# In-projection summed over two halves of K instead of four quarters, with the modulation tiles reordered to match

## The chip, the cores and the metric

The kernel runs on one core of a Trainium2 chip. Its time is the device time of one execution in microseconds. The five engines run side by side and meet through semaphores: TensorE (PE in the rows), VectorE (DVE), ScalarE (ACT), GpSimd (POOL) and SyncE (SP), which here only issues DMAs.

## What is computed

One layer of a hybrid encoder with S = 256 tokens and D = 2048, batch 1, all in float32. The parts that matter here:

```python
c_act = jax.nn.silu(c)
mod = c_act @ w_ada[l] + b_ada[l]                       # (1, 6 * 2048)
sh_a, sc_a, g_a, sh_m, sc_m, g_m = [m[:, None, :] for m in jnp.split(mod, 6, axis=-1)]
h = rms_norm(x, norm_mix[l]) * (1.0 + sc_a) + sh_a
p = h @ w_in[l]                                         # the in-projection, K = 2048
...                                                     # latent projections, three attentions
x = x + g_a * (o @ w_out[l])
h = rms_norm(x, norm_ffn[l]) * (1.0 + sc_m) + sh_m
x = x + g_m * (jnp.square(jax.nn.relu(h @ w_ff1[l])) @ w_ff2[l])
```

## The kernel before

Every large weight comes as **units** of 128 x 1024 floats (512 KB): two K tiles by 512 columns. Four buffers (`RING`) hold raw units, four their high parts, four their low parts. SP loads a unit into `raw`; ACT (`hi`, L334) rounds it to `w_hi`; VectorE (`lo`, L594) subtracts to get `w_lo`; TensorE (`unit`, L975 and L981) multiplies `w_hi` with the high and low half of the operand and `w_lo` with the high half, 24 matmuls, and counts `unit_used`. ACT may overwrite `w_hi` of a unit once TensorE has used the unit four before it, and SP may overwrite `raw` once VectorE has done `lo` of the unit four before it (`lo_done`).

The modulation vector `mod` isn't made by TensorE. VectorE makes it from `w_ada`, in 192 **tiles** of 128 x 1024 (`ada_tile`, L606), each a multiply by `c_rep` (silu(c) on all partitions) and a sum along the row; two tiles give one column of `mod`. The tiles too pass through four buffers (`ADA`): SP may load tile a once tile a - 4 is done (`ada_done`), and VectorE waits for the tile's landing (`ada_full`). VectorE takes the tiles in a fixed order, between its other work. Tiles 0 to 63 are scale and shift of the mixer, 64 to 95 the mixer's gate (first needed behind the out-projection), the rest belongs to the MLP.

An operand **pair** is two K tiles of h, and needs eight tiles of `mod`: `mix_gain` and `norm_t` on VectorE (L625, L636), `mix_hi` on ACT (L360), `norm_lo` on VectorE (L647).

The **in-projection** has 64 units. K is cut into four quarters; for each quarter q there are eight column blocks b of two units. TensorE sums a block's two units in PSUM (two sets, used in turn) and VectorE adds the block to `pT` (`read_block`, L662, L663; a copy in the first quarter). Quarter q needs operand pairs 2q and 2q + 1. Ahead of the loop stand 16 tiles and two pairs (the **head**); each block carries two tiles, and pairs 2q + 2 and 2q + 3 are made in blocks 4 and 7 of quarter q. The loop thus takes 64 tiles, and 16 are left to the **latent projections** (10 units, seven blocks).

Each engine has one queue, in the order in which the functions below write it. SP's is the one that sets when loads start: a DMA whose semaphore isn't there yet holds all that stand behind it. What it waits for is in these lines:

```python
def load_unit(u):
    slot = u % RING
    if u >= RING:
        sp.wait_ge(lo_done, u - RING + 1)
def load_ada(a):
    slot = a % ADA
    if a >= ADA:
        sp.wait_ge(ada_done, a - ADA + 1)
```

Of the kernel before, what the change touches and what calls it, by code (L numbers as in the profile page):

```python
# [22 lines left out]
P = 128  # L23
D, S, FF = 2048, 256, 8192
EPS = 1e-6
KT = D // P
# [7 lines left out]
RING = 4  # L34
LAG = RING
AHEAD = LAG + RING
# [15 lines left out]
ADA = 4  # L52
SH_A, SC_A, G_A, SH_M, SC_M, G_M = range(6)


QT = KT // 4
QC = KT
A_GA, A_SHM, A_SCM, A_GM, A_END = 64, 96, 128, 160, 192


# [7 lines left out]

USE_XS = 0
USE_IN = 1  # L70
USE_LSTAT = 33
USE_LAT = 34
USE_ROT, USE_VM, USE_VS = 41, 42, 43
USE_OT = 44
USE_OUT = 46
USE_FFN = 50
USE_FF1A, USE_FF2A, USE_FF1B, USE_FF2B, USE_END = 51, 59, 63, 71, 75

READY = {use: n + 1 for n, use in enumerate((
    USE_XS, USE_LSTAT, USE_ROT, USE_VM, USE_VS, USE_OT, USE_OT + 1, USE_FFN, USE_END))}  # L80
# [2 lines left out]
R_MIX, R_CQ, R_CKV, R_O, R_FFN = 0, 8, 10, 11, 19  # L83
# [43 lines left out]
def hybrid_block(nc, xt_in, cols_in, consts_in, w_ada, weights, c_row, out):  # L127
    ctx = ExitStack()
    with ctx:
# [130 lines left out]
        @block.sync  # L260
        def _(sp):
# [4 lines that stand above are left out]
                sp.dma_start(raw[:, slot, :, :].rearrange("p k n -> p (k n)"),  # L266
                             weights[u, :, :]).then_inc(raw_full[slot], 16)
# [5 lines that stand above are left out]
                sp.dma_start(ada[:, slot, :], w_ada[a, :, :]).then_inc(ada_full[slot], 16)  # L273

            sp.dma_start(cols[:, :], cols_in).then_inc(ld_cols, 16)
            load_ada(0)
            sp.dma_start(xT[:, :, :].rearrange("p k t -> p (k t)"), xt_in).then_inc(ld_x, 16)
            load_ada(1)
            load_ada(2)
            for a in range(3, ADA):  # L280
                load_ada(a)
            for u in range(RING):
                load_unit(u)
            for a in range(8):
                load_ada(a + ADA)
            load_unit(RING)
            load_unit(RING + 1)
            for a in range(8, 12):
                load_ada(a + ADA)
            load_unit(RING + 2)  # L290
            load_unit(RING + 3)
            for a in range(12, 16):
                load_ada(a + ADA)

            for q in range(4):
                if q == 3:
                    sp.dma_start(consts[:, :], consts_in).then_inc(ld_const, 16)
                for b in range(8):
                    load_unit(QC * q + AHEAD + 2 * b)
                    load_unit(QC * q + AHEAD + 2 * b + 1)  # L300
                    for a in range(2):
                        load_ada(16 * (q + 1) + 2 * b + a + ADA)

            loaded = AHEAD
            for n in range(7):
                for u in range(loaded, LAT_ENDS[n] + 1 + AHEAD):
                    load_unit(B_LAT + u)
                loaded = LAT_ENDS[n] + 1 + AHEAD
                for a in range(2):
                    load_ada(A_GA + 16 + 2 * n + a + ADA)  # L310
            for a in range(A_GA + 30, A_SCM):
                load_ada(a + ADA)

            for j in range(U_OUT):
                load_unit(B_OUT + AHEAD + j)
                load_ada(A_SCM + j + ADA)
            for j in range(UNITS - B_FF - AHEAD):
                load_unit(B_FF + AHEAD + j)
                if j % 2 == 1 and A_GM + j // 2 + ADA < A_END:
                    load_ada(A_GM + j // 2 + ADA)  # L320
            for j in range(4):
                sp.wait_ge(result_ready, 4 * j + 4)
                src = (tmp, tmp2, sq, ssq)[j]
                sp.dma_start(out[:, 4 * j * S:(4 * j + 4) * S], scratch(src)).then_inc(ld_out, 16)
            sp.wait_ge(ld_out, 64)

        @block.scalar
        def _(sc):
            def hi(u0, step, it, j):
                slot = (u0 + j) % RING  # L330
                sc.wait_ge(raw_full[slot], 16 * ((u0 + j) // RING + 1) + (16 * step // RING) * it)
                if u0 + j >= RING:
                    sc.wait_ge(unit_used, u0 + j - RING + 1 + step * it)
                sc.activation(w_hi[:, slot, :, :], raw[:, slot, :, :], ACT.Copy).then_inc(hi_done, 1)  # L334
# [44 lines left out]
            def mix_hi(j):  # L379

                sc.wait_ge(ada_done, 8 * j + 8)
                operand_hi(R_MIX + j, hT[:, 2 * j:2 * j + 2, :, :], mod[:, SH_A, 2 * j:2 * j + 2])

            mix_hi(0)
            mix_hi(1)
            for q in range(4):
                for b in range(8):
                    hi(QC * q + LAG, 0, 0, 2 * b)
                    hi(QC * q + LAG, 0, 0, 2 * b + 1)
                    if q < 3 and b == 4:  # L390
                        mix_hi(2 * q + 2)
                if q < 3:
                    mix_hi(2 * q + 3)

            sc.wait_ge(part_done, 32)
            for i, n in ((0, 4), (1, 2)):
                if i:
                    sc.wait_ge(cq_summed, 1)
# [125 lines left out]
        def _(gp):  # L524
# [5 lines left out]
            gp.wait_ge(zeroed, 1)  # L530
            for b in range(4):
                add_squares(b + 1)
            gp.wait_ge(part_done, 32)
            gp.memset(foxA[:, :], 0.0).then_inc(fox_filled, 1)
            gp.memset(foxG[:, :], 0.0).then_inc(fox_filled, 1)
            gp.wait_ge(fox_filled, 2)
# [53 lines left out]
        def _(ve):  # L590
            def lo(u):
                slot = u % RING
                ve.wait_ge(hi_done, u + 1)
                ve.tensor_tensor(w_lo[:, slot, :, :], raw[:, slot, :, :],  # L594
                                 w_hi[:, slot, :, :].bitcast(F32), ALU.subtract).then_inc(lo_done, 1)
# [56 lines left out]
            def norm_t(r0, j):  # L652
                scaled_pair(r0 + j, xT[:, 2 * j:2 * j + 2, :], gain[:, 2 * j:2 * j + 2], 0)

            def norm_lo(r0, shift, j):
                operand_lo(r0 + j, hT[:, 2 * j:2 * j + 2, :, :], mod[:, shift, 2 * j:2 * j + 2])
# [35 lines left out]
            def mix_gain(j):  # L692
                make_gain(SC_A, C_MIX, 2 * j, 2, 8 * j + 7)
                ve.wait_ge(gain_ready, j + 1)

            for a in range(8):
                ada_tile(a)
            lo(0)
# [5 lines left out]
            ada_tile(8)  # L704
            ada_tile(9)
            invert(1, 1)
            mix_gain(0)
            norm_t(R_MIX, 0)
            ada_tile(10)
            norm_lo(R_MIX, SH_A, 0)  # L710
            ada_tile(11)
            lo(2)
            lo(3)
            for a in range(12, 16):
                ada_tile(a)
            mix_gain(1)
            norm_t(R_MIX, 1)
            norm_lo(R_MIX, SH_A, 1)

            for q in range(4):  # L720
                for b in range(8):
                    u = QC * q + 2 * b
                    lo(u + LAG)
                    lo(u + LAG + 1)
                    ada_tile(16 * (q + 1) + 2 * b)
                    ada_tile(16 * (q + 1) + 2 * b + 1)
                    if q < 3 and b == 4:
                        mix_gain(2 * q + 2)
                        norm_t(R_MIX, 2 * q + 2)
                    if q < 3 and b == 5:  # L730
                        norm_lo(R_MIX, SH_A, 2 * q + 2)
                    if q < 3 and b == 7:
                        mix_gain(2 * q + 3)
                        norm_t(R_MIX, 2 * q + 3)
                    if q:
                        ve.wait_ge(part_done, 8 * (q - 1) + b + 1)
                    read_block(pT[:, 4 * b:4 * b + 4, :], USE_IN + 8 * q + b, u + 2, add=q > 0).then_inc(part_done, 1)
                    ve.wait_ge(part_done, 8 * q + b + 1)
                    ve.sem_inc(psum_free, 1)
                    if q < 3 and b == 7:  # L740
                        norm_lo(R_MIX, SH_A, 2 * q + 3)

            ve.wait_ge(psum_ready, READY[USE_LSTAT])
            mean(USE_LSTAT, 0, 0, QL)
# [27 lines left out]
            for n, e in enumerate(LAT_ENDS):  # L772
                for u in range(LAG if n == 0 else LAT_ENDS[n - 1] + 1 + LAG, e + 1 + LAG):
                    lo(B_LAT + u)
                ada_tile(A_GA + 16 + 2 * n)
                ada_tile(A_GA + 16 + 2 * n + 1)
                read_block(dests[n], USE_LAT + n, B_LAT + e + 1).then_inc(psum_free, 1)
            ada_tile(A_GA + 30)
            ada_tile(A_GA + 31)
            ve.wait_ge(psum_free, USE_LAT + 8)  # L780

            cos, sin = consts[:, K_COS:K_COS + S], consts[:, K_SIN:K_SIN + S]
# [177 lines left out]
        def _(pe):  # L960
# [47 lines left out]
            pe.wait_ge(ld_cols, 16)  # L1008
            pe.wait_ge(ssq_done, 4)
            token_sums(USE_XS, 1, ssq, 4).then_inc(psum_ready, 1)  # L1010
            for q in range(4):
                for b in range(8):
                    product(QC * q + 2 * b, 2, USE_IN + 8 * q + b, hT, QT * q, lambda j: (op_lo, R_MIX + 2 * q + j + 1))
            take(USE_LSTAT)
            pe.wait_ge(sq_done, 5)
            token_sums(USE_LSTAT, 0, tmp2, 4).then_inc(cq_summed, 1)
# [191 lines left out]
```

## Time and profile before

| | us |
|---|---|
| median of 3 runs | 1302.89 (1298.74 to 1304.67) |
| the profiled execution | 1298.17 |
| its span, first to last instruction | 1296.4 |
| head, until the loop starts | 54.65 |
| in-projection loop | 54.65 to 283.3 |
| latent projections, statistics ahead of them included | 283.3 to 345.5 |
| TensorE busy | 1139.5 (88%) |
| VectorE busy | 903.8 (70%) |

The shares of the span are means over stages with different limits, so the stages are to be read one by one. Times in the rows are microseconds from the start of the span, durations in the last brackets are idle time of the engine ahead of that row and who ended it. A line such as "x2" joins instructions of one kind that follow one another.

### The profile page before, as it was taken

The numbers are of one execution on the slowest core, as the hardware profiler recorded it, in microseconds if no ns is written. First come the engines' busy times: TensorE is split into PE (matmuls) and PEld (weight loads), VectorE is DVE, ScalarE is ACT, GpSimd is POOL, SyncE is SP. The second block draws the span as 40 slices with busy tenths as digits, with TensorE's granted clock in tenths as the row PEclk, the third lists the DMA queues.
The fourth block names the chain that finished last, engine by engine and source line by source line (L and its number), as shares of the span: only waits on it lengthen the run. The fifth ranks groups of instructions, "written<-read, shape, count | busy, mean of one in ns | idle before, by whom it ended". The sixth has DMA issues, their size and how long they took to land.

```text
span 1296.4 us, 22085 instructions
## 1 busy us (share of the span) xinstructions
PE 1139.5 (88%) x9186; PEld 1097.1 (85%) x9186; DVE 903.8 (70%) x1172; ACT 523.0 (40%) x619; POOL 87.1 (7%) x86
## 2 busy tenths in 40 slices
PE   1497888867698969959999999999999999999996
PEld 0487877866566659949999999999999999999996
DVE  4797989878879988888777765444455555554554
ACT  3132323324167633335444443333345444444441
POOL 3000000000026520010000000000000000000000
PEclk9898989888858779979999999999999999999998
DMA  8797979884744438975878766666665666666661
GB/s 308 273 325 254 322 264 326 304 296 151 271 146 149 156 112 330 369 298 197 309 275 307 278 211 194 195 193 196 189 193 193 198 192 196 195 193 197 194 192 71
DMA packets 81170, 298.49 MB, mean 230 GB/s; under 512 B 9136, under 2 KB 9264, under 8 KB 80688
## 3 DMA queue, kind: packets, MB, share of 16 engines
q1 hardware_dynamic: 80784, 296.03, 67.6%
q8 instruction: 73, 1.20, 0.4%
q10 hardware_dynamic: 288, 1.06, 0.2%
q14 instruction: 25, 0.20, 0.0%
HBM read 294.94 MB, written 2.11 MB: 229 GB/s over the span
## 4 chain that ended last, share of the span: by engine, by line
PE 65%; DVE 22%; issue 7%; ACT 3%; DMA 2%; POOL 1%; DVEq 0%; ACTq 0%; POOLq 0%
PE ps L975 41%; PE ps L981 20%; DVE ada L606 10%; DVE w_lo L594 4%; DVE pT L662 2%; PE ps L1064 2%; ACT w_hi L334 1%; DMA c_rep<-c_row 1%; DVE pT L663 1%; DVE tmp L636 1%; DMA c_row<-c_act 1%; DVE rstd L619 1%; DVE hT L647 1%; DVE stick L830 0%; PE ps L1005 0%
## 5 line engine op out<-in xcount | busy, mean ns | idle before, releaser
L594 DVE TENSOR_TENSOR w_lo<-raw,w_hi 128x1024 fp32r<-128x1024 f32 x362 | 446.3, 1246 | 305.9 <-ACT w_hi L334 301.4
L334 ACT ACTIVATE w_hi<-raw 128x1024 fp32r<-128x1024 f32 x362 | 380.5, 1059 | 526.0 <-PE ps L981 496.3
L975 PE MATMUL ps<-hT,w_hi 128*128 128x256 f32 x3584 | 457.7, 281 | 60.4 <-DVE hT L647 22.0
L975 PEld LDWEIGHTS ps<-hT,w_hi 128*128 128x128 f32 x3584 | 433.9, 192 | 68.3 <-DVE hT L647 22.8
L975 PE MATMUL ps<-act,w_hi 128*128 128x256 f32 x2048 | 252.9, 276 | 0.0
L981 PE MATMUL ps<-hT,w_lo 128*128 128x256 f32 x1792 | 242.6, 278 | 0.4 <-DVE w_lo L594 0.4
L975 PEld LDWEIGHTS ps<-act,w_hi 128*128 128x128 f32 x2048 | 241.6, 188 | 0.0
L981 PEld LDWEIGHTS ps<-hT,w_lo 128*128 128x128 f32 x1792 | 222.9, 190 | 0.6 <-DVE w_lo L594 0.6
L981 PE MATMUL ps<-act,w_lo 128*128 128x256 f32 x1024 | 136.9, 276 | 0.0
L981 PEld LDWEIGHTS ps<-act,w_lo 128*128 128x128 f32 x1024 | 125.6, 188 | 0.0
L606 DVE CUSTOM_DVE_ANT_0 ada<-ada,c_rep,half_sum 128x1024 f32<-128x1024 f32 x96 | 123.8, 1307 | 0.3 <-DMA ada<-in_ada 0.3
L606 DVE CUSTOM_DVE_ANT_0 ada<-ada,c_rep,cols 128x1024 f32<-128x1024 f32 x64 | 84.1, 1324 | 0.0
L527 POOL TENSOR_TENSOR ssq<-ssq,sq 128x1024 f32<-128x1024 f32 x10 | 25.4, 2539 | 753.3 <-ACT sq L340 739.1
L606 DVE CUSTOM_DVE_ANT_0 ada<-ada,c_rep,plus_one 128x1024 f32<-128x1024 f32 x32 | 40.8, 1276 | 15.2 <-DMA c_rep<-c_row 15.0
L562 POOL TENSOR_TENSOR tmp<-o_tok 128x64 f32<-128x64 f32 (+1 forms) x48 | 35.7, 764 | 18.4 <-DVE o_tok L844 13.2
L975 PE MATMUL ps<-lat,w_hi 128*128 128x256 f32 x160 | 23.7, 306 | 14.8 <-issue 7.3
L975 PEld LDWEIGHTS ps<-lat,w_hi 128*128 128x128 f32 x160 | 21.9, 209 | 16.1 <-issue 7.6
L930 DVE TENSOR_TENSOR act<-tmp,act 128x1024 fp32r<-128x1024 f32 x16 | 19.6, 1225 | 18.1 <-ACT act L502 18.1
L502 ACT ACTIVATE act<-tmp 128x1024 fp32r<-128x1024 f32 x16 | 17.0, 1062 | 33.8 <-DVE tmp L924 33.8
L360 ACT ACTIVATE hT<-tmp,mod 128x256 fp32r<-128x256 f32 x16 | 8.1, 508 | 54.0 <-DVE tmp L636 54.0
L662 DVE TENSOR_TENSOR pT<-pT,ps 128x1024 f32<-128x1024 f32 x24 | 29.2, 1215 | 0.0
L994 PE MATMUL ps<-ssq,cols 128*128 128x256 f32 x8 | 3.8, 650 | 27.0 <-POOL ssq L527 27.0
(141 smaller groups left out, 625.5 us busy)
## 6 DMA issues: line engine op xcount, KB each, us to landing
raw<-in_weights SPq DMA_DIRECT2D x362, 512.0 KB, 4.4
ada<-in_ada SPq DMA_DIRECT2D x192, 512.0 KB, 5.2
xT<-in_xt SPq DMA_DIRECT2D x1, 2048.0 KB, 8.5
consts<-in_consts SPq DMA_DIRECT2D x1, 1156.0 KB, 8.1
c_rep<-c_row ACTq DMA_DIRECT2D x1, 1024.0 KB, 8.1
y<-tmp SPq DMA_DIRECT2D x2, 512.0 KB, 2.6
y<-sq SPq DMA_DIRECT2D x1, 512.0 KB, 2.6
y<-ssq SPq DMA_DIRECT2D x1, 512.0 KB, 2.6
```

Source lines behind the costliest of these rows:

```text
L334: sc.activation(w_hi[:, slot, :, :], raw[:, slot, :, :], ACT.Copy).then_inc(hi_done, 1)
L502: sc.activation(act[:, 4 * b + 8 * it:4 * b + 8 * it + 4, 0, :], tmp2[:, :, :], ACT.Copy).then_inc(act_hi, 1)
L527: gp.tensor_tensor(ssq[:, :, :], ssq[:, :, :], sq[:, :, :], ALU.add).then_inc(ssq_done, 1)
L562: ins = gp.tensor_tensor(osq[i % 2][:, q * d:q * d + d], o, o, ALU.mult)
L594: ve.tensor_tensor(w_lo[:, slot, :, :], raw[:, slot, :, :], w_hi[:, slot, :, :].bitcast(F32), ALU.subtract).then_inc(lo_done, 1)
L606: ve.tensor_tensor_reduce(out=ada[:, slot, :], in0=ada[:, slot, :], scale=1.0, scalar=first, in1=c_rep[:, half * D // 2:(half + 1) * D // ...
L619: ve.reciprocal(rstd[:, 0:halves, :], rstd[:, 0:halves, :]).then_inc(rstd_ready, 1)
L662: return ve.tensor_tensor(dst, dst, set_of(use), ALU.add)
L930: ve.tensor_tensor(act[:, 4 * it:4 * it + 4, 1, :], tmp2[:, :, :], act[:, 4 * it:4 * it + 4, 0, :].bitcast(F32), ALU.subtract).then_inc(ac ...
L975: pe.matmul(acc[:, n, :], w, rhs[:, kt0 + k, half, :], start=first and k == 0 and n % 2 == 0 and half == 0, stop=False, skip_group_check=True)
L981: ins = pe.matmul(acc[:, n, :], w_lo[:, slot, k, n * P:(n + 1) * P], rhs[:, kt0 + k, 0, :], start=False, stop=last and k == UK - 1, skip_g ...
L1064: ins = pe.matmul(s[:, q * P:(2 * q + 1) * P], lhs[:, q * P:(q + 1) * P], rhs[:, 0:(q + 1) * P], start=(m == 0), stop=(m == len(terms) - 1))
```

## The change

QT, the K tiles of a part, goes from 4 to 8: the in-projection has two halves of eight column blocks, and a block sums four units in PSUM ahead of its read. The first half needs pairs 0 to 3, so the head now has 32 tiles and four pairs; pairs 4 to 7 are made in blocks 1, 3, 5 and 7 of the first half. A block carries four tiles, one behind each unit's subtraction. The loop takes tiles 32 to 95, so none is left in the latent projections. The host packs the weights in two parts, and the counters follow.

```diff
-QT = KT // 4
-QC = KT
+QT = KT // 2
+QC = 2 * KT
@@ SP
-            for a in range(8):
+            for a in range(28):
                 load_ada(a + ADA)
-            load_unit(RING)
-            load_unit(RING + 1)
-            for a in range(8, 12):
-                load_ada(a + ADA)
-            load_unit(RING + 2)
-            load_unit(RING + 3)
-            for a in range(12, 16):
-                load_ada(a + ADA)
-
-            for q in range(4):
-                if q == 3:
+                if a % 7 == 6:
+                    load_unit(RING + a // 7)
+
+            for q in range(2):
+                if q == 1:
                     sp.dma_start(consts[:, :], consts_in).then_inc(ld_const, 16)
                 for b in range(8):
-                    load_unit(QC * q + AHEAD + 2 * b)
-                    load_unit(QC * q + AHEAD + 2 * b + 1)
-                    for a in range(2):
-                        load_ada(16 * (q + 1) + 2 * b + a + ADA)
+                    for j in range(4):
+                        load_unit(QC * q + AHEAD + 4 * b + j)
+                        load_ada(32 * (q + 1) + 4 * b + j)
...
-                for a in range(2):
-                    load_ada(A_GA + 16 + 2 * n + a + ADA)
-            for a in range(A_GA + 30, A_SCM):
+            for a in range(A_SHM - ADA, A_SCM):
                 load_ada(a + ADA)
@@ ACT
-            mix_hi(0)
-            mix_hi(1)
-            for q in range(4):
+            for j in range(4):
+                mix_hi(j)
+            for q in range(2):
                 for b in range(8):
-                    hi(QC * q + LAG, 0, 0, 2 * b)
-                    hi(QC * q + LAG, 0, 0, 2 * b + 1)
-                    if q < 3 and b == 4:
-                        mix_hi(2 * q + 2)
-                if q < 3:
-                    mix_hi(2 * q + 3)
+                    for j in range(4):
+                        hi(QC * q + LAG, 0, 0, 4 * b + j)
+                    if q == 0 and b % 2 == 1:
+                        mix_hi(4 + b // 2)
@@ VectorE
-            for a in range(12, 16):
-                ada_tile(a)
-            mix_gain(1)
-            norm_t(R_MIX, 1)
-            norm_lo(R_MIX, SH_A, 1)
-
-            for q in range(4):
+            for j in range(1, 4):
+                for a in range(8 * j + (4 if j == 1 else 0), 8 * j + 8):
+                    ada_tile(a)
+                mix_pair(j)
+                norm_lo(R_MIX, SH_A, j)
+
+            for q in range(2):
                 for b in range(8):
-                    u = QC * q + 2 * b
-                    lo(u + LAG)
-                    lo(u + LAG + 1)
-                    ada_tile(16 * (q + 1) + 2 * b)
-                    ada_tile(16 * (q + 1) + 2 * b + 1)
...
+                    u = QC * q + 4 * b
+                    for j in range(4):
+                        lo(u + LAG + j)
+                        ada_tile(32 * (q + 1) + 4 * b + j)
+                    if q == 0 and b % 2 == 1:
+                        mix_pair(4 + b // 2)
...
-                    read_block(pT[:, 4 * b:4 * b + 4, :], USE_IN + 8 * q + b, u + 2, add=q > 0).then_inc(part_done, 1)
+                    read_block(pT[:, 4 * b:4 * b + 4, :], USE_IN + 8 * q + b, u + 4, add=q > 0).then_inc(part_done, 1)
...
-                ada_tile(A_GA + 16 + 2 * n)
-                ada_tile(A_GA + 16 + 2 * n + 1)
                 read_block(dests[n], USE_LAT + n, B_LAT + e + 1).then_inc(psum_free, 1)
-            ada_tile(A_GA + 30)
-            ada_tile(A_GA + 31)
@@ TensorE
-                    product(QC * q + 2 * b, 2, USE_IN + 8 * q + b, hT, QT * q, lambda j: (op_lo, R_MIX + 2 * q + j + 1))
+                    product(QC * q + 4 * b, 4, USE_IN + 8 * q + b, hT, QT * q, lambda j: (op_lo, R_MIX + 4 * q + j + 1))
```

**SP's queue, from the end of the head into the loop.** Before (the last row is the first pair of tile loads of the loop, tiles 20 and 21; w_ada tiles go to `ada`, units to `raw`):

```order
L273 DMA ada<-in_ada 128x1024 [waits ada_done] x8
L266 DMA raw<-in_weights 128x1024 [waits lo_done] x2
L273 DMA ada<-in_ada 128x1024 [waits ada_done] x4
L266 DMA raw<-in_weights 128x1024 [waits lo_done] x2
L273 DMA ada<-in_ada 128x1024 [waits ada_done] x4
L266 DMA raw<-in_weights 128x1024 [waits lo_done] x2
L273 DMA ada<-in_ada 128x1024 [waits ada_done] x2
```

Now, the same place (the "x7" rows end the head with tile 31; the "x2" is unit 7 of the head and unit 8 of the loop, and the row behind it is tile 32):

```order
L273 DMA ada<-in_ada 128x1024 [waits ada_done] x7
L266 DMA raw<-in_weights 128x1024 [waits lo_done]
L273 DMA ada<-in_ada 128x1024 [waits ada_done] x7
L266 DMA raw<-in_weights 128x1024 [waits lo_done] x2
L273 DMA ada<-in_ada 128x1024 [waits ada_done]
L266 DMA raw<-in_weights 128x1024 [waits lo_done]
L273 DMA ada<-in_ada 128x1024 [waits ada_done]
```

What moved: the head loads 32 tiles instead of 20, and in the loop one unit and one tile alternate, where two and two did.

**VectorE's queue, one block of the loop.** Before (the first block; ISA rows are the tiles of `mod`, the row of 128x1 behind each is its sum read out):

```order
L594 TENSOR_TENSOR w_lo<-raw,w_hi 128x1024 [waits hi_done] x2
L606 ISA ada,half_sum<-ada,c_rep,plus_one 128x1024 [waits ada_done,ada_full0]
L606 ISA half_sum 128x1
L606 ISA ada,half_sum<-ada,c_rep,cols 128x1024 [waits ada_done,ada_full1]
L606 ISA half_sum 128x1
L663 COPY pT<-ps1 128x1024 [waits unit_used]
```

Now, the first block of the first half (the first ISA row is tile 32; L583 and L595 are the old L594 and L606):

```order
L583 TENSOR_TENSOR w_lo<-raw,w_hi 128x1024 [waits hi_done]
L595 ISA ada,half_sum<-ada,c_rep,plus_one 128x1024 [waits ada_done,ada_full0]
L595 ISA half_sum 128x1
L583 TENSOR_TENSOR w_lo<-raw,w_hi 128x1024 [waits hi_done]
L595 ISA ada,half_sum<-ada,c_rep,cols 128x1024 [waits ada_done,ada_full1]
L595 ISA half_sum 128x1
L583 TENSOR_TENSOR w_lo<-raw,w_hi 128x1024 [waits hi_done]
L595 ISA ada,mod<-ada,c_rep,half_sum 128x1024 [waits ada_done,ada_full2]
L595 ISA mod 128x1
L583 TENSOR_TENSOR w_lo<-raw,w_hi 128x1024 [waits hi_done]
L595 ISA ada,mod<-ada,c_rep,half_sum 128x1024 [waits ada_done,ada_full3]
L652 COPY pT<-ps1 128x1024 [waits unit_used]
```

What moved: a tile now follows each subtraction, and the read comes after four units instead of two.

## Rows read from the trace of the kernel before

**Rows 1.** Windows: stretch, length, busy by engine (instructions), clock, DMA share, GB/s

```profile
core 0: us, PE busy (x) PEld busy (x) DVE busy (x) ACT busy (x) POOL busy (x), PEclk, DMA share, GB/s
...
54.65:113.00 58.35, 48.51 (x384) 46.93 (x384) 50.94 (x67) 18.46 (x20) 0.00 (x0) 0.94 0.83 292
...
229.90:283.30 53.40, 44.85 (x360) 43.48 (x360) 47.18 (x56) 15.92 (x15) 0.00 (x0) 0.95 0.91 323
...
305.50:345.50 40.00, 28.99 (x200) 26.41 (x198) 36.71 (x46) 10.48 (x10) 2.87 (x2) 0.91 0.84 293
...
540.00:550.00 10.00, 10.00 (x90) 10.00 (x90) 9.88 (x16) 2.21 (x3) 0.00 (x0) 1.00 1.02 411
```

**Rows 2.** Timeline, one block on VectorE and SP: start, duration, engine, line

```profile
66.23 2.36 DVE L594 TENSOR_TENSOR w_lo<-raw,w_hi 128x1024 fp32r<-128x1024 f32 x2
68.51 1.28 DVE L606 CUSTOM_DVE_ANT_0 ada<-ada,c_rep,half_sum 128x1024 f32<-128x1024 f32 x1
...
70.93 1.22 DVE L663 COPY pT<-ps 128x1024 f32<-128x1024 f32 x1
72.29 2.36 DVE L594 TENSOR_TENSOR w_lo<-raw,w_hi 128x1024 fp32r<-128x1024 f32 x2
...
73.54 1.46 SPq L266 DMA_DIRECT2D raw<-in_weights  x2
```

**Rows 3.** Waits from 60 to 283: us in total, times, longest

```profile
DVE w_lo L594 <- ACT w_hi L334: 24.3, 7, 5.8
...
PE ps L975 <- DVE hT L647: 15.3, 3, 5.1
```

**Rows 4.** Timeline, seam between the first and the second quarter

```profile
109.72 0.08 DVE L606 DVE_READ_ACCUMULATOR2_ANT mod<- 128x1 f32 x1
...
110.83 1.22 DVE L663 COPY pT<-ps 128x1024 f32<-128x1024 f32 x1
...
113.00 1.21 DVE L594 TENSOR_TENSOR w_lo<-raw,w_hi 128x1024 fp32r<-128x1024 f32 x1
...
113.13 3.78 PE L975 MATMUL ps<-hT,w_hi 128*128 128x256 f32 x16 [5.04 <-DVE hT L647]
...
118.97 1.06 ACT L334 ACTIVATE w_hi<-raw 128x1024 fp32r<-128x1024 f32 x1 [6.10 <-PE ps L981]
```

**Rows 5.** Timeline, last pair of the head and the loop's first subtraction

```profile
51.48 0.08 DVE L606 DVE_READ_ACCUMULATOR2_ANT mod<- 128x1 f32 x1
...
54.65 1.23 DVE L594 TENSOR_TENSOR w_lo<-raw,w_hi 128x1024 fp32r<-128x1024 f32 x1
```

**Rows 6.** Timeline, the only tile that waited for its load in the head

```profile
31.83 1.28 DVE L606 CUSTOM_DVE_ANT_0 ada<-ada,c_rep,half_sum 128x1024 f32<-128x1024 f32 x1 [0.26 <-DMA ada<-in_ada]
```

**Rows 7.** Single loads: issue duration in ns, when, and time to landing

```profile
L266 SPq DMA_DIRECT2D raw<-in_weights x1: 327/327/327, 121.3 to 121.3; - x1
...
DMA to landing us min/median/max: 3.4/3.4/3.4
...
L273 SPq DMA_DIRECT2D ada<-in_ada x1: 328/328/328, 122.5 to 122.5; - x1
...
DMA to landing us min/median/max: 4.4/4.4/4.4
...
L273 SPq DMA_DIRECT2D ada<-in_ada x1: 328/328/328, 368.9 to 368.9; - x1
...
L273 SPq DMA_DIRECT2D ada<-in_ada x1: 328/328/328, 370.9 to 370.9; - x1
...
DMA to landing us min/median/max: 3.9/3.9/3.9
```

**Rows 8.** Timeline, three issues in a row on SP at the start

```profile
2.12 1.42 SPq L273 DMA_DIRECT2D ada<-in_ada  x3
```

**Rows 9.** Timeline, last read of the in-projection

```profile
282.12 1.22 DVE L662 TENSOR_TENSOR pT<-pT,ps 128x1024 f32<-128x1024 f32 x1
```

More of the change, by code:

```diff
@@ L70 @@
 USE_IN = 1
[L71 to L77, printed above, removed]
+USE_LSTAT = 17
+USE_LAT = 18
+USE_ROT, USE_VM, USE_VS = 25, 26, 27
+USE_OT = 28
+USE_OUT = 30
+USE_FFN = 34
+USE_FF1A, USE_FF2A, USE_FF1B, USE_FF2B, USE_END = 35, 43, 47, 55, 59
 READY = {use: n + 1 for n, use in enumerate((
@@ L382, in mix_hi @@
                 operand_hi(R_MIX + j, hT[:, 2 * j:2 * j + 2, :, :], mod[:, SH_A, 2 * j:2 * j + 2])
-            mix_hi(0)
-            mix_hi(1)
-            for q in range(4):
+            for j in range(4):
+                mix_hi(j)
+            for q in range(2):
                 for b in range(8):
-                    hi(QC * q + LAG, 0, 0, 2 * b)
-                    hi(QC * q + LAG, 0, 0, 2 * b + 1)
-                    if q < 3 and b == 4:
-                        mix_hi(2 * q + 2)
-                if q < 3:
-                    mix_hi(2 * q + 3)
-            sc.wait_ge(part_done, 32)
+                    for j in range(4):
+                        hi(QC * q + LAG, 0, 0, 4 * b + j)
+                    if q == 0 and b % 2 == 1:
+                        mix_hi(4 + b // 2)
+            sc.wait_ge(part_done, 16)
             for i, n in ((0, 4), (1, 2)):
@@ L532, in _ @@
                 add_squares(b + 1)
-            gp.wait_ge(part_done, 32)
+            gp.wait_ge(part_done, 16)
             gp.memset(foxA[:, :], 0.0).then_inc(fox_filled, 1)
@@ L694, in mix_gain, with mix_pair @@
                 ve.wait_ge(gain_ready, j + 1)
+            def mix_pair(j):
+                mix_gain(j)
+                norm_t(R_MIX, j)
             for a in range(8):
@@ L706, in _ @@
             invert(1, 1)
-            mix_gain(0)
-            norm_t(R_MIX, 0)
+            mix_pair(0)
             ada_tile(10)
@@ L713, in _ @@
             lo(3)
-            for a in range(12, 16):
-                ada_tile(a)
-            mix_gain(1)
-            norm_t(R_MIX, 1)
-            norm_lo(R_MIX, SH_A, 1)
-            for q in range(4):
-                for b in range(8):
-                    u = QC * q + 2 * b
-                    lo(u + LAG)
-                    lo(u + LAG + 1)
-                    ada_tile(16 * (q + 1) + 2 * b)
-                    ada_tile(16 * (q + 1) + 2 * b + 1)
[L727 to L734, printed above, removed]
+            for j in range(1, 4):
[4 more added lines that the diff above has]
+            for q in range(2):
+                for b in range(8):
+                    u = QC * q + 4 * b
[4 more added lines that the diff above has]
+                        mix_pair(4 + b // 2)
                     if q:
-                        ve.wait_ge(part_done, 8 * (q - 1) + b + 1)
-                    read_block(pT[:, 4 * b:4 * b + 4, :], USE_IN + 8 * q + b, u + 2, add=q > 0).then_inc(part_done, 1)
+                        ve.wait_ge(part_done, b + 1)
+                    read_block(pT[:, 4 * b:4 * b + 4, :], USE_IN + 8 * q + b, u + 4, add=q > 0).then_inc(part_done, 1)
                     ve.wait_ge(part_done, 8 * q + b + 1)
                     ve.sem_inc(psum_free, 1)
-                    if q < 3 and b == 7:
-                        norm_lo(R_MIX, SH_A, 2 * q + 3)
+                    if q == 0 and b % 2 == 1:
+                        norm_lo(R_MIX, SH_A, 4 + b // 2)
             ve.wait_ge(psum_ready, READY[USE_LSTAT])
@@ L1010, in _ @@
             token_sums(USE_XS, 1, ssq, 4).then_inc(psum_ready, 1)
-            for q in range(4):
+            for q in range(2):
                 for b in range(8):
-                    product(QC * q + 2 * b, 2, USE_IN + 8 * q + b, hT, QT * q, lambda j: (op_lo, R_MIX + 2 * q + j + 1))
+                    product(QC * q + 4 * b, 4, USE_IN + 8 * q + b, hT, QT * q, lambda j: (op_lo, R_MIX + 4 * q + j + 1))
             take(USE_LSTAT)
@@ L1178 @@
     ukv = w_ukv.reshape(KVL, H, NOPE + VD)
-    parts = [w_in[q * QT * P:(q + 1) * QT * P] for q in range(4)]
+    parts = [w_in[q * QT * P:(q + 1) * QT * P] for q in range(2)]
     parts += [
```

## The prediction

> **What bounds the kernel now.** I read the windows by stage first, then who waited for whom, then the timeline of one block, then how long single loads take to land.
>
> In the in-projection VectorE is the busy engine: 50.9 of 58.4 us in the first quarter, 47.2 of 53.4 in the last, while TensorE has 48.5 and 44.8 [rows 1]. The timeline of one block says why: two w_lo subtractions (66.23 to 68.51, 2.28 us), two modulation tiles (68.51 to 70.93, 1.21 us each) and one read of PSUM with its bookkeeping (70.93 to 72.29, 1.36 us), 6.06 us for two units with no gap [rows 2]. So a tile or a subtraction taken from VectorE there is a gain at its full price, and anything VectorE is made to wait for is a loss at its full price. The one other cost is the seam between quarters: TensorE waits 5.1 us for the operand of the next quarter, three times 15.3 us in all, and VectorE then waits 5.8 us at most for ACT's w_hi, which waits for TensorE's first unit at low clock [rows 3, 4]. VectorE never waits for a tile's DMA in this stage: no such line stands among its waits, since every tile is asked for when the fourth tile before it is done.
>
> **The change part by part.** I go along VectorE, since the end follows it until the latent projection is over, and then add what each stage gives or takes.
>
> *Head.* Before, 16 tiles and 2 operand pairs stand ahead of the loop; now 32 and 4. A tile is 1.21 us [rows 2], eight are 9.7. A pair (gain, norm, wait for ACT, low part) runs from 51.48 to 54.65, 3.17 us [rows 5]. The ring has four tile buffers, so the fifth tile of a run is asked for when the first is done, 3 x 1.21 = 3.6 us before its turn, and a load takes 3.8 us or more; the only such case before shows 0.26 us of waiting [rows 6], and with 4.4 to 5 us to landing it would be about 1.2 for a run of eight. One extra round is 9.7 + 3.2 + 1.2 = 14.1, two are **+28 us** (26 without any waiting, 30 with slow loads). Nothing hides it: TensorE has no more than four units to do until VectorE enters the loop.
>
> *The in-projection as written.* Sixteen blocks of four units, each 4 subtractions, 4 tiles, 1 read: 16 reads fewer than now, 16 x 1.36 = 21.8 us. The seams go too: the four later pairs are ready before the second half starts, so the three waits of 5 to 6 us vanish. If the tiles were there in time, a block would be 4 x 1.15 + 4 x 1.21 + 1.36 = 10.8 us, and this would be a clear gain. The order on SP says that they aren't. Before, the loop asked for tile n + 4 in the round that uses tile n. Now the head has asked for tiles 4 to 31 and no further, and the loop has no lead left: SP waits for subtraction 4 + 4b + j, issues a weight unit, and right behind it the load of tile 32 + 4b + j, which is the tile VectorE takes up directly after that same subtraction. The buffers of the four older tiles have long been free, so the load could have gone earlier; it is the weight load ahead of it on SP's queue, with its wait for lo_done, that holds it. VectorE executes in order, so the next subtraction, which would release SP again, stands behind the tile. Subtraction, load, tile are thus one closed chain, 64 times.
>
> Its length per unit:
> - subtraction started to the weight load's issue: 72.29 to 73.54, 1.25 us [rows 2];
> - weight issue to tile issue: an issue takes 0.33 us [rows 7], three in a row took 1.42, so 0.47 each [rows 8]; I take 0.40;
> - tile issue to landing: the trace has no pair 0.4 us apart. A load with nothing in flight takes 3.4 us; one issued 1.2 us behind it 4.4; one 1.9 us behind 3.9 [rows 7]. The closer, the longer: 0.5 us more for 0.7 us closer, so another 0.5 to 0.6 at 0.4 us. I take 4.9. It can't be under 3.4 (alone); the upper end is 5.3, if the second always lands 2.2 us behind the first, as at 1.2 us apart (122.5 + 4.4 against 121.3 + 3.4);
> - landing to the tile's start: a few hundredths, 0.03;
> - tile to the next subtraction: 1.21 [rows 2].
>
> Sum 7.79 us a unit, where now 6.06 / 2 = 3.03 and the seams stand. 64 x 7.79 = 498.6; 16 reads x 1.36 = 21.8; four pairs in the first half, each 1.11 us ahead of the read (109.72 to 110.83) and 0.81 behind it (from 110.83 + 1.36 to 113.00) [rows 4], 7.6. Together 528.0 us, against 228.7 now, from the loop's start at 54.65 [rows 5] to the end of its last read at 283.34 [rows 9]: **+299 us**. None of this is hidden, since ACT, TensorE and the weight loads are all ahead of VectorE: a weight unit is still asked for four units before its use, some 30 us, and even at the low clock a unit costs TensorE under 5.8 us (started at 113.13, ACT released by its end at 118.97) [rows 4], less than 7.79. The clock may well fall in the long gaps; it would cost the sum nothing.
>
> A rule of the Trainium skill bears on the landing term. The trace shows 3.4 us alone and, 1.2 us apart, 5.6 us from the first issue to the second landing [rows 7]. DMA: Bandwidth & Descriptors, section "Anatomy of one DMA — SWDGE (gpsimd) path", fits about 2.0 us plus the bytes over 436 GB/s, for another issuing path. By it one load of 512 KB is 3.2 us and two at once land 4.4 us after the first issue, so the tile 4.0 us after its own, and the sum would be 64 x 0.9 = 58 us lower, 1559 us. The rows lie above it, more so for two loads than for one, so I stay at 4.9.
>
> *The latent projection* loses all its 16 tiles. VectorE is busy 36.7 of 40.0 us there, TensorE 29.0 [rows 1]; without 14 tiles (17 us) TensorE is the bound and the stage shrinks by about 40 - 29 = 11. The last two stand between the last read of PSUM and the rotary product, 2 x 1.21 = 2.4 us. **-13 us** (at least 9, at most 16 x 1.21 = 19). The first tiles of the attention are now asked for behind the last weight loads of this stage, some 12 us ahead of their use, so they cost nothing. What follows is the same work in the same order.
>
> **Sum.** 28 + 299 - 13 = +314. The profiled span of 1296.4 becomes 1610; the median shown (1302.9) lies 6.5 us above that span, so I expect a median of **1617 us**.
>
> **The rivals.**
> *The tile's load costs less than I think.* If the pair of loads lands almost like one, the term is 3.5 instead of 4.9: 64 x 1.4 = 90 us less, 1527. For it: the engines move 411 GB/s over 10 us when many loads are under way [rows 1]. Against it: every close pair in rows 7 shows the second one later. Page and rows together leave this about one chance in eight, spread over 1527 to 1565.
> *It costs more.* With four loads in flight landings of over 6 us occur; at 6.3 the sum is 90 us more, 1706. But here the DMA is empty at each pair, so this is unlikely: 4 in 100.
> *The other side, faster.* Loads keep ahead of VectorE after all. The deciding point is whether a tile's load is issued a whole block, or at least 5 us, before VectorE reaches it. Then 16 x 10.8 + 7.6 = 180.4 us stand against 228.7, -48; with +28 and -13 that is -33, 1270 us. It asks 4.19 MB in 10.8 us, 388 GB/s, and the trace shows 411 [rows 1], so the DMA would allow it. The order on SP speaks against it: the wait for lo_done ahead of each tile's load is in the program. 3 in 100, for a slip in my count of tiles.
> On that rival the skill has a sentence of its own: the same page, section "Where 436 GB/s comes from", puts HBM at about 358 GB/s per core; a block would then be 11.7 us and the time 1284, still faster.
>
> **How the numbers follow.** My forecast has 0.81, the cheap landing 0.12, the dear one 0.04, the faster case 0.03. The forecast's own ends are a landing of 4.3 (a full transfer behind the first at stream rate; -38) and 5.3 (+26), and the head and the latent stage add 2 and 5 either way: 1574 to 1649. To hold 8 in 10 I widen it a little into both landings, 1565 to 1655. A measurement of this kernel can tell 0.5% from no change; slower by more than that has 0.96, faster 0.03, within it 0.01.
>
> **What would show it.** VectorE's tile group (L595 in the new numbering) waits for DMA ada<-in_ada 64 times for about 5.4 us each, some 350 us in total, where now it waits once [rows 6]; GB/s fall to about half in the in-projection (1.05 MB in 7.8 us); the chain that ended last names DMA for about a fifth of the span; TensorE's clock is low in much of the in-projection; 16 reads fewer; the loop starts near 83 us. In the latent stage TensorE waits less for VectorE. I am wrong if those waits are absent (then the faster rival), if they are 4.7 us or less (the cheap landing), or if VectorE waits for ACT's w_hi instead, which would make TensorE's low clock the bound.

## The result, and the profile of the changed kernel

| | before | after |
|---|---|---|
| median, us | 1300.82 (1297.48 to 1304.67, 4 runs) | 1599.03 (1595.99 to 1626.25, 4 runs) |
| span of the profiled execution, us | 1296.4 | 1597.0 |

The changed kernel takes 1.228 times as long (95% interval 1.223 to 1.234). The forecast was 1617 us, 1565 to 1655.

In the profiles of three kernels below (E1, E5 and E7) the feed-forward part ran some 20 us longer than elsewhere (541.9 instead of 521.5 us for the same matmuls), so I read their in-projection loops from the profile and the totals of E1 and E7 from their timed runs.

Windows of the changed kernel, by stage (stretch, length, busy by engine, clock, DMA share, GB/s), the answer to [rows 1]: the end of the head, the loop, the latent projections.

```profile
54.70:85.60 30.90, 9.96 (x48) 9.56 (x48) 24.82 (x44) 3.37 (x8) 0.00 (x0) 0.61 0.79 290
85.60:594.30 508.70, 254.83 (x1464) 242.22 (x1464) 182.37 (x228) 68.39 (x71) 0.00 (x0) 0.70 0.38 135
594.30:645.90 51.60, 39.23 (x258) 35.36 (x258) 31.32 (x35) 19.02 (x22) 4.04 (x6) 0.81 0.29 93
```

Look at the middle row. VectorE works 182 of 509 us, TensorE 255, the DMA engines 38%: no engine is near full, so the stage must be bound by something that passes from one to the next. The waits of VectorE in that stretch have a single line (total, times, longest):

```profile
DVE ada L595 <- DMA ada<-in_ada: 323.8, 64, 6.5
```

182.4 busy and 323.8 waiting are 506.2 of the 508.7 us. In the loop before, VectorE waited for no tile at all. The other end of the same chain shows in what SP waits for. Before, in the loop:

```profile
SPq L266 <- DVE w_lo L594: 130.7, 64, 6.7
SPq L273 <- DVE half_sum L606: 27.5, 32, 0.9
SPq L273 <- DVE mod L606: 26.5, 32, 0.9
```

After, in the loop:

```profile
SPq L266 <- DVE w_lo L583: 458.3, 64, 10.5
```

Before, a tile's load waited (shortly) for the buffer of an older tile: the queue ran ahead and was held back by space. After, no tile's load waits for anything; all the waiting is at the unit's load in front of it. One round on VectorE and SP shows the links:

```profile
302.34 1.22 DVE L583 TENSOR_TENSOR w_lo<-raw,w_hi 128x1024 fp32r<-128x1024 f32 x1
303.58 0.33 SPq L266 DMA_DIRECT2D raw<-in_weights  x1
...
303.96 0.43 SPq L273 DMA_DIRECT2D ada<-in_ada  x1
...
308.31 1.28 DVE L595 CUSTOM_DVE_ANT_0 ada<-ada,c_rep,half_sum 128x1024 f32<-128x1024 f32 x1 [4.75 <-DMA ada<-in_ada]
309.52 0.08 DVE L595 DVE_READ_ACCUMULATOR2_ANT mod<- 128x1 f32 x1
309.52 1.22 DVE L652 COPY pT<-ps 128x1024 f32<-128x1024 f32 x1
```

Subtraction at 302.34, unit issued 1.24 later, tile issued 0.38 behind it, VectorE at the tile 4.35 later, 1.21 for the tile: 7.18 us for a unit. The chain that ended last now runs through the tiles' loads, for 20% of the span; before, the DMA had 2% of it:

```profile
PE 54%; DMA 21%; DVE 14%; issue 8%; SPq 1%; ACT 1%; POOL 0%; DVEq 0%; ACTq 0%; POOLq 0%
PE ps L956 32%; DMA ada<-in_ada 20%; PE ps L962 16%; DVE w_lo L583 6%; DVE ada L595 3%; PE ps L1045 3%; SPq L266 1%; DVE pT L652 1%; DVE pT L651 1%; PE ps L1055 1%; DMA c_row<-c_act 1%; DMA c_rep<-c_row 0%; ACT w_hi L325 0%; PE ps L975 0%; DVE tmp L625 0%
```

By stage, span against span: the loop starts at 85.63 instead of 54.65, +31.0; it lasts 508.7 instead of 228.7, +280.0; from its last read to the rotary product it is 51.6 instead of 64.5, -12.9; all behind that 951.0 instead of 948.6, +2.5. Together 300.6, the whole difference of the spans.

### The profile page after: what moved, and what is told of

It reads as the page before. It is cut to its first block, busy times and chain, and to the rows that moved or that the text cites. A ratio compares the mean times of both kernels' runs of the same rounds, so it can differ in the third digit from the quotient of the medians.

```text
span 1597.0 us, 22037 instructions
## 1 busy us (share of the span) xinstructions
PE 1217.7 (76%) x9186; PEld 1167.2 (73%) x9186; DVE 891.3 (56%) x1156; ACT 522.3 (33%) x619; POOL 87.0 (5%) x86
## 4 chain that ended last, share of the span: by engine, by line
PE 54%; DMA 21%; DVE 14%; issue 8%; SPq 1%; ACT 1%; POOL 0%; DVEq 0%; ACTq 0%; POOLq 0%
PE ps L956 32%; DMA ada<-in_ada 20%; PE ps L962 16%; DVE w_lo L583 6%; DVE ada L595 3%; PE ps L1045 3%; SPq L266 1%; DVE pT L652 1%; DVE pT L651 1%; PE ps L1055 1%; DMA c_row<-c_act 1%; DMA c_rep<-c_row 0%; ACT w_hi L325 0%; PE ps L975 0%; DVE tmp L625 0%
## 5 line engine op out<-in xcount | busy, mean ns | idle before, releaser
L956 PE MATMUL ps<-hT,w_hi 128*128 128x256 f32 x3584 | 499.2, 297 | 143.0 <-DVEq L724 57.8
L583 DVE TENSOR_TENSOR w_lo<-raw,w_hi 128x1024 fp32r<-128x1024 f32 x362 | 448.7, 1246 | 284.7 <-ACT w_hi L325 282.4
L956 PEld LDWEIGHTS ps<-hT,w_hi 128*128 128x128 f32 x3584 | 477.4, 209 | 148.8 <-DVEq L724 84.5
L962 PE MATMUL ps<-hT,w_lo 128*128 128x256 f32 x1792 | 273.2, 300 | 123.0 <-DVE w_lo L583 123.0
L962 PEld LDWEIGHTS ps<-hT,w_lo 128*128 128x128 f32 x1792 | 247.2, 208 | 132.0 <-DVE w_lo L583 132.0
L595 DVE CUSTOM_DVE_ANT_0 ada<-ada,c_rep,half_sum 128x1024 f32<-128x1024 f32 x96 | 125.4, 1309 | 160.2 <-DMA ada<-in_ada 160.2
L595 DVE CUSTOM_DVE_ANT_0 ada<-ada,c_rep,cols 128x1024 f32<-128x1024 f32 x64 | 84.8, 1326 | 125.1 <-DMA ada<-in_ada 125.0
L595 DVE CUSTOM_DVE_ANT_0 ada<-ada,c_rep,plus_one 128x1024 f32<-128x1024 f32 x32 | 40.9, 1278 | 58.9 <-DMA ada<-in_ada 42.5
L975 PE MATMUL ps<-tmp,cols 128*128 128x256 f32 x12 | 5.8, 658 | 37.4 <-ACT tmp L388 37.4
L975 PEld LDWEIGHTS ps<-tmp,cols 128*128 128x128 f32 x12 | 3.7, 328 | 39.1 <-issue 36.9
```

The lines of the kernel that those rows point to most:

```text
L583: ve.tensor_tensor(w_lo[:, slot, :, :], raw[:, slot, :, :], w_hi[:, slot, :, :].bitcast(F32), ALU.subtract).then_inc(lo_done, 1)
L595: ve.tensor_tensor_reduce(out=ada[:, slot, :], in0=ada[:, slot, :], scale=1.0, scalar=first, in1=c_rep[:, half * D // 2:(half + 1) * D // ...
L956: pe.matmul(acc[:, n, :], w, rhs[:, kt0 + k, half, :], start=first and k == 0 and n % 2 == 0 and half == 0, stop=False, skip_group_check=True)
L962: ins = pe.matmul(acc[:, n, :], w_lo[:, slot, k, n * P:(n + 1) * P], rhs[:, kt0 + k, 0, :], start=False, stop=last and k == UK - 1, skip_g ...
```

## The experiments

My theory is that the order on SP alone costs the time: each tile is asked for only when VectorE has come to it. The rivals are that the four-unit blocks and TensorE's low clock are slow by themselves, and that the DMA can't carry the loads of a denser loop.

**E1. Give back the lead.** The changed kernel, tiles loaded four ahead:

```diff
-            for a in range(28):
+            for a in range(32):
                 load_ada(a + ADA)
-                if a % 7 == 6:
+                if a % 7 == 6 and a < 28:
                     load_unit(RING + a // 7)
...
-                        load_ada(32 * (q + 1) + 4 * b + j)
+                        load_ada(32 * (q + 1) + 4 * b + j + 4)
...
-            for a in range(A_SHM - ADA, A_SCM):
+            for a in range(A_SHM - ADA + 4, A_SCM):
```

> The changed kernel with one edit on SP: tiles are again loaded four ahead of their use (the head loads tiles 4 to 35, the loop loads tile n + 4 where it loaded tile n). My theory, that SP asks for each tile only when VectorE has come to it: the 64 waits of 4.4 to 4.9 us are gone, the loop goes from 509 us to about 180 (16 blocks of 10.8 us and 7.6 for four pairs), and the time is about 1270 us, 2.4% under the kernel before. First rival, that the four-unit blocks and TensorE's low clock make the loop slow whatever the tiles do: over 1500 us. Second rival, that DMA cannot carry the 4.19 MB of a block in 10.8 us (388 GB/s): VectorE waits for tiles or ACT for units, a block is 11.7 us or more, and the time is 1285 or more.

Measured: 1267.5 us (1264.0 to 1291.5, 5 runs), 0.973 of before (0.968 to 0.978). The loop before and the loop of E1, by windows:

```profile
54.65:283.30 228.65, 190.53 (x1512) 184.40 (x1512) 199.98 (x254) 71.30 (x75) 0.00 (x0) 0.94 0.85 297
...
84.55:264.60 180.05, 170.75 (x1464) 170.19 (x1464) 177.28 (x228) 68.99 (x71) 0.00 (x0) 0.96 0.98 374
```

The second is 180.05 us, the 180 of the theory, with VectorE busy 177.3 of them and without a wait for a tile. Nothing in the blocks or in TensorE was touched, and the 329 us are gone, so the first rival falls. The second falls too, though narrowly: the DMA share is 0.98 at 374 GB/s. Landings have risen, as this answer for the tiles of the loop shows, but with four tiles of lead a tile has 9.4 us or more from its issue to its turn on VectorE, four rounds of 2.35:

```profile
DMA to landing us min/median/max: 4.5/6.2/7.2
```

**E2. One tile of lead.** The same with 1 in place of 4 (head to 29, + 1, + 1).

> The changed kernel, tiles loaded one ahead instead of none. By my theory the closed chain (subtraction ends, SP issues unit and tile 0.5 us later, tile lands 4.4 us later, tile, next subtraction) now spans two units instead of one, so a unit takes 7.3 / 2 = 3.65 us, or 3.9 if landings rise to 5 us with more in flight; the loop takes 235 to 265 us and the kernel 1325 to 1355. By the rival that blames the four-unit blocks it stays over 1500. By one that blames DMA bandwidth rather than order, one tile of lead changes little and it stays near 1600.

Measured: 1360.0 us in one run, 5 us over the upper end. The loop is 272.6 us against 180.05 and 508.7. Its window, and the waits of VectorE for tiles:

```profile
85.60:358.20 272.60, 195.03 (x1464) 189.89 (x1464) 181.12 (x228) 68.42 (x71) 0.00 (x0) 0.87 0.70 251
...
DVE ada L595 <- DMA ada<-in_ada: 88.8, 44, 4.3
```

One tile of lead takes almost three quarters of the cost away, as a chain closed over two units instead of one should. Its landings are 4.8 us in the median, between the two values that the expectation took. What its lower end left out are the reads and the pairs: they stand in the chain too. Two units take 1.24 + 0.38 + 4.8 + 0.04 + 1.21 = 7.67 us, so 64 take 245, and with 29 us for 16 reads and four pairs it is 275 (an estimate from these terms), against 272.6 measured.

**E3. The tile's load ahead of the unit's.** The same waits, only the two issues change places:

```diff
+                        sp.wait_ge(lo_done, QC * q + AHEAD + 4 * b + j - RING + 1)
+                        load_ada(32 * (q + 1) + 4 * b + j)
                         load_unit(QC * q + AHEAD + 4 * b + j)
-                        load_ada(32 * (q + 1) + 4 * b + j)
```

> The changed kernel, same waits, but of each pair of loads the tile's is issued ahead of the unit's. It prices the landing by itself. If a tile lands later because a unit's load stands 0.4 us ahead of it: the tile lands 3.5 us after its issue instead of 4.4 and its issue comes 0.4 us earlier, a unit takes 6.0 us instead of 7.2, the loop 413 us instead of 509, the kernel about 1505. If the unit's load has no part in it (4.4 us is what a tile takes at this pace): only the 0.4 us of issue go, 24 us, and the kernel takes about 1575.

Measured: 1507.5 us in one run, the loop 422.4 us. Its window, and one round of 6.01 us, from tile to tile:

```profile
85.30:507.70 422.40, 239.05 (x1464) 228.09 (x1464) 182.43 (x228) 68.35 (x72) 0.00 (x0) 0.73 0.46 162
...
304.47 1.28 DVE L596 CUSTOM_DVE_ANT_0 ada<-ada,c_rep,cols 128x1024 f32<-128x1024 f32 x1 [3.52 <-DMA ada<-in_ada]
...
310.48 1.28 DVE L596 CUSTOM_DVE_ANT_0 ada<-ada,c_rep,cols 128x1024 f32<-128x1024 f32 x1 [3.58 <-DMA ada<-in_ada]
```

Tiles land in 3.5 us in the median here and in 4.4 us in the changed kernel. Of the 7.2 us of a usual round, then, 1.2 are the unit's load in front: some 0.4 from its issue to the tile's, and some 0.9 by which the tile lands later behind it. The order of two issues on one queue is worth 86 us in the loop.

**E4. Quarters without lead.** The kernel before, with only the lead of the tiles taken away in the loop:

```diff
-            for a in range(12, 16):
-                load_ada(a + ADA)
...
-                        load_ada(16 * (q + 1) + 2 * b + a + ADA)
+                        load_ada(16 * (q + 1) + 2 * b + a)
...
+            for a in range(ADA):
+                load_ada(A_GA + 16 + a)
             loaded = AHEAD
```

> The kernel before with its quarters, its two-unit blocks and its head, but the loop loads tile n in the round that uses tile n, as the changed kernel does; the four tiles of lead come back behind the loop. By my theory each of the 32 blocks waits once for its first tile (0.5 us of issue and about 5 to land, behind two units) and a little for the second: 5.5 to 6 us, 175 to 190 in all, some of it in place of the waits at the three seams: 1460 to 1490 us. By the rival that blames the halves: about 1300, as before.

Measured: 1510.5 us in one run, 20 us over the range. So the halves aren't needed for the loss; the missing lead makes it with quarters as well, 210 us in the loop (438.7 against 228.7). What I under-priced is the landing: with two units and two tiles issued within some 2 us, the tiles of this loop land in 6.5 us in the median, and VectorE waits 206.4 us for them:

```profile
54.70:493.40 438.70, 247.46 (x1512) 241.11 (x1512) 204.14 (x254) 71.15 (x75) 0.00 (x0) 0.75 0.47 159
...
DVE ada L606 <- DMA ada<-in_ada: 206.4, 34, 8.5
...
DVE w_lo L594 <- ACT w_hi L334: 23.7, 7, 5.9
```

The last line is the seams, still there at nearly the price that they had before (24.3 in [rows 3]).

**E5. Half of TensorE's work.** The changed kernel, 12 matmuls a unit instead of 24 in the in-projection, so that the low half of the operand and half of w_lo's products are left out there:

```diff
-                        for half in range(2):
+                        for half in range(1 if u < U_IN else 2):
...
-                for k in range(UK):
+                for k in range(UK - 1 if u < U_IN else 0, UK):
                     for n in range(4):
                         ins = pe.matmul(acc[:, n, :], w_lo[:, slot, k, n * P:(n + 1) * P], rhs[:, kt0 + k, 0, :],
```

> The changed kernel with half of TensorE's work left out in the in-projection: each unit there takes 8 matmuls of w_hi with the operand's high half and 4 of w_lo, 12 instead of 24. It tests whether TensorE, which shows a granted clock of 0.70 in the loop and is busy half of it, has any part in the loop's 509 us. My theory, that VectorE's closed chain of subtraction, load and tile sets the pace alone: the loop still takes 505 to 511 us and the kernel 1590 to 1603. Rival, that TensorE at its low clock delays ACT's w_hi and so the subtractions: 12 matmuls fewer of 0.11 to 0.23 us each in 64 units are 85 to 175 us of work, so 1425 to 1515 us.

Measured: 1610.2 us in one run, 7 us over the expected range, with the longer feed-forward part named above in it; the loop is 496.8 us, 8 us under the expected 505 to 511 and far from the rival's, which would be 85 to 175 us shorter than 509:

```profile
86.40:583.20 496.80, 170.38 (x732) 154.08 (x732) 182.46 (x228) 68.34 (x72) 0.00 (x0) 0.56 0.38 138
```

TensorE is busy 170 instead of 255 us, its clock is lower still (0.56), and the loop loses 12 us, all of them in VectorE's waits for tiles:

```profile
DVE ada L595 <- DMA ada<-in_ada: 311.8, 64, 6.2
```

VectorE never waits for w_hi in either loop, so TensorE's pace and clock have no part in it. The 12 us have another source, which the last section tells.

**E6. Two tiles of lead.** As E1 with 2 in place of 4.

> The changed kernel, tiles loaded two ahead. Landings were 4.4 us with no lead, 4.8 with one tile, 6.3 with four, where the DMA engines are 98% busy. With two tiles of lead a landing may take (0.5 us of issue) + L = 3 x 2.36 - 1.2 us before VectorE waits, so L up to 5.4 us. If landings are 5.2 to 5.4: no waits, loop 180 us, time 1267, as with four. If they are near 6, each unit pays about 0.2 to 0.3 us, 13 to 20 us in all: 1280 to 1288. Under 1265 nothing that I know of would explain it.

Measured: 1296.3 us (median of 10 runs, nine from 1290.7 to 1321.2 and one of 2886.9), 0.993 of before (0.991 to 0.996), 8 us over the expected 1280 to 1288; the loop 207.3 us. The landings are 5.8 us in the median and up to 7.7, and the waits are back in part:

```profile
84.70:292.00 207.30, 178.32 (x1464) 177.19 (x1464) 179.98 (x228) 68.77 (x71) 0.00 (x0) 0.92 0.90 327
...
DVE ada L595 <- DMA ada<-in_ada: 24.1, 27, 2.9
```

I expected 13 to 20 us for landings of 6 us and it is 27. The expectation had the time too long that two tiles of lead give: it took 0.5 us of issue off a stretch that begins with the subtraction, but the tile is issued 1.62 us behind the subtraction's start. From the issue to the tile's turn there are 2 x 2.35 + 1.14 - 1.62 = 4.2 us where no read falls between, not 5.4. Followed round by round with this in place, landings of 5.8 us alike for all tiles give a loop of 206 us, and each tile's own landing gives 208 (estimates from these terms): the spread of the landings adds little. Two tiles of lead are too few for landings of this length, four are enough.

**E7. Four tiles of lead again.**

> The kernel with four tiles of lead once more, for its profile and beside the one with two: 1267 us, loop 180 us, with VectorE busy 177 of them and no wait of VectorE for a tile in the loop.

Measured: 1270.8 us (1264.7 to 1292.2, 4 runs), 0.975 of before (0.970 to 0.981). Its loop ran 180.3 us, without a wait of VectorE for a tile:

```profile
84.93:265.24 180.31, 171.33 (x1464) 170.77 (x1464) 177.41 (x228) 69.00 (x71) 0.00 (x0) 0.96 0.98 373
```

This kernel is faster than the changed one and, by 2 to 3%, than the one before, and the two sets of runs agree.

## Why the prediction was right, point by point

- **The mechanism** holds as it was put: subtraction, load and tile are one closed chain, 64 times. VectorE waits 64 times, for 323.8 us (forecast: 64 times, some 350). E1 and E4 show it from both sides: with the lead given back, the changed kernel has no such wait; with the lead taken away, the old one has 206 us of them.
- **The length of the chain** was the term that was off: 7.79 us a unit forecast, 7.2 in most rounds and 7.5 in the mean. The issue terms hold (1.25 and 0.40 forecast, 1.24 and 0.38 measured); the landing was 4.9, and is 4.4 in the median, 4.2 to 6.0. I had drawn a line through two pairs of [rows 7] and prolonged it to a distance of 0.4 us: the closer, the later. That doesn't hold here. The two loads land 1.25 us apart when they are issued 0.4 us apart (3.6 and 4.4 in the median, 0.4 between the issues), not the 1.9 that the line gave. The value is close to the lower end of my range, 4.3, a full transfer behind the first. By the median alone the landing is 31 us too dear in the sum. Luck gave 14 us of it back: ten landings are 1.4 us late (last section), for which the forecast had no term. The mean landing is 4.6 us, and the loop comes out at 508.7 instead of 528, 19 us less; that is the miss of 18 us, since the other differences nearly cancel (head +3, behind the rotary product +2.5 where I had nothing, and the median stands 2.0 us above the span, not 6.5).
- **How near the cheap landing was.** I had called myself wrong if VectorE's waits were 4.7 us or less. The mean is 5.06, but the median is 4.8: the usual round is nearer to that rival than the total suggests. The lower end of the range, 1574, should also have been 1572 by its own terms.
- **The rule of the Trainium skill** (DMA: Bandwidth & Descriptors, "Anatomy of one DMA — SWDGE (gpsimd) path") gives an estimate of 3.2 us for one load and 4.0 for this landing. Both are too low for loads issued on SP, as the rows had said: 3.5 with nothing ahead (E3), 4.4 behind a unit.
- **The gain of the halves** is real and was sized right, only hidden under the loss: with the lead, the loop is 180.05 us against the 180.4 of the faster rival, and E1's 1267.5 against its 1270. Of the 48.6 us that E1's loop is shorter than the old one, VectorE's busy time gives 22.7 (200.0 to 177.3, 16 reads above all) and its idle time 25.9 (28.7 to 2.8, the seams). The rival's second price, 1284 us from 358 GB/s, doesn't hold here: E1's loop moved 374 GB/s.
- **The head** costs 31.0 us, 28 forecast. 1.5 of the 3 are there when the second pair is done, since VectorE starts 1.2 us later (it waits 16.1 us for c_rep, 15.0 before) and waits 0.4 us more for one tile. In the two rounds behind it the waits for tiles are 3.1 us, six of them, where I had put 2.4; the last 0.8 is in shorter gaps.
- **The latent projections** give 12.9 us, 13 forecast. VectorE is busy 20.2 of the last 27.4 us and TensorE 24.3, so TensorE is the busier one there, as forecast; but the 29 us that I had taken for its floor are 24.3 at a granted clock of 1.00 (0.91 before), so the close agreement is in part luck.
- **TensorE's clock** fell to 0.70 in the loop and cost the sum nothing (E5).

## What to carry to other kernels

When a loop's counters are renumbered, lay the issuing queue's order beside the consumer's order and count, for each load, how many of its kind are issued before the one in use: no lead means that every load's full time to landing is paid. On a queue that is served in order it isn't the load's own wait that matters but the wait of whatever stands in front of it. Size the lead by the landing time of the busy loop (6.2 us in E1, 7.2 at most), not of the quiet one (3.5), and count the time that it gives from the load's issue, not from the round's start: 4.2 us with two tiles here, 9.4 with four.

## What the runs showed of the hardware

**Landing time grows with what is in flight.** For 512 KB on SP's queue, in the median: 3.5 us with nothing ahead (E3), 4.4 with one load 0.4 us ahead, 4.8 and 5.8 with one and two tiles of lead, 6.2 (E1) and 5.9 (E7) with four at 98% DMA share, and 6.5 in E4, where four loads are issued within some 2 us although the engines are busy only 47% of the time. A burst of four is as bad here as a loop at 98%.

**Some landings are late by 1.4 us, together with a fetch of instructions.** Ten of the 64 tiles in the changed kernel's loop took over 5 us. Here is one, issued at 118.8, and the DMA queues from its issue to its landing:

```profile
L273 SPq DMA_DIRECT2D ada<-in_ada x1: 431/431/431, 118.8 to 118.8; - x1
...
DMA to landing us min/median/max: 5.8/5.8/5.8
```

```profile
q1 hardware_dynamic: 288, 1.05, 56.1%
q8 instruction: 1, 0.02, 1.0%
```

A packet of queue q8 (instruction, 16 KB) falls into the flight of all ten late tiles, while of the 54 others one has a packet in its flight and still lands after 4.4 us. The loop has 12 packets of q8 in all, E5's loop has 6 with half the matmuls, and there 5 tiles are late:

```profile
q8 instruction: 12, 0.20, 0.1%
```

```profile
q8 instruction: 6, 0.10, 0.1%
```

Five late tiles fewer at 1.4 us are 7 of the 12 us by which E5's loop is shorter; a median landing of 4.3 instead of 4.4 us is about the rest. E3's loop has 12 packets too: ten fall into a tile's flight, and five of these ten tiles are its only late ones (5.0 to 5.4 us), while the other five land after 3.4 to 3.7 us. That the fetch delays the landing is what these counts suggest; no run moved a fetch by itself, so it isn't shown.
